# Stick-breaking attention: suffix sums as one-pass products of a rounded part and its remainder, scores with 128 rows of weights, first two heads begun among the projections

## The reference

```python
z = jnp.einsum('bhqd,bshd->bhqs', q_blk, k) * d ** -0.5
causal = key_pos[None, :] < q_pos[:, None]
log_beta = jax.nn.log_sigmoid(z)
log_1m_beta = jnp.where(causal, jax.nn.log_sigmoid(-z), 0.0)
between = lax.cumsum(log_1m_beta, axis=3, reverse=True) - log_1m_beta
w = jnp.where(causal, jnp.exp(log_beta + between), 0.0)
return jnp.einsum('bhqs,bshd->bqhd', w, v)
```

## Time and profile before

| | us |
|---|---|
| median of 3 runs (2274.93 to 2283.06) | 2282.37 |
| the profiled execution | 2286.35 |
| its span | 2284.5 |
| TensorE busy | 2074.4 |
| VectorE busy | 1025.5 |
| ScalarE busy | 756.0 |
| GpSimd busy | 160.6 |
| granted TensorE clock, mean (1 is 2.4 GHz) | 0.94 |

### The profile page before, as it was taken

The page is one execution under the profiler, slowest core; times in us unless marked ns, Lnnn a source line. Parts: engine busy times, 40 slices in busy tenths (PEclk is TensorE's granted clock), DMA queues, the critical chain, the costliest instruction groups (busy, mean ns, idle before and its releaser), DMA issues.

```text
span 2284.5 us, 25379 instructions
## 1 busy us (share of the span) xinstructions
PE 2074.4 (91%) x9952; PEld 1680.9 (74%) x9952; DVE 1025.5 (45%) x1428; ACT 756.0 (33%) x1130; POOL 160.6 (7%) x179
## 2 busy tenths in 40 slices
PE   7999899999998989999999979895459788999898
PEld 6855678887887777788887868683359566888786
DVE  5322534334246554333343345556533437666534
ACT  3134432222235445322223241424213224333322
POOL 3000010000003110100000050000012021000000
PEclk9989899999999998899999989997579899999998
DMA  6200023222222010222222323020020022332231
GB/s 188 93 19 1 19 74 110 92 92 92 93 85 71 27 56 1 76 92 92 92 93 91 101 67 100 1 92 19 19 56 1 1 74 74 99 97 98 74 108 38
DMA packets 140699, 158.09 MB, mean 69 GB/s; under 512 B 15944, under 2 KB 129616, under 8 KB 140624
## 3 DMA queue, kind: packets, MB, share of 16 engines
q1 hardware_dynamic: 139328, 155.01, 21.5%
q0 software_dynamic: 1296, 2.05, 0.3%
HBM read 153.36 MB, written 3.68 MB: 69 GB/s over the span
## 4 chain that ended last, share of the span: by engine, by line
PE 86%; DVE 8%; ACT 2%; issue 2%; POOL 1%; DMA 1%; SPq 0%; DVEq 0%; ACTq 0%; POOLq 0%
PE bank L2373 30%; PE bank L2027 16%; PE bank L2394 16%; PE bank L2051 3%; PE bank L2114 3%; PE bank L2142 2%; PE bank L2239 2%; PE bank L2130 1%; PE bank L2352 1%; PE bank L2227 1%; POOL arena L774 1%; PE bank L2250 1%; PE bank L2562 1%; PE bank L2288 1%; PE bank L2185 1%
## 5 line engine op out<-in xcount | busy, mean ns | idle before, releaser
L2373 PE MATMUL bank<-XH,w_hi 128*128 128x512 f32 x1008 | 398.5, 395 | 0.8 <-DVE w_lo L1569 0.8
L2373 PE MATMUL bank<-XH,w_lo 128*128 128x512 f32 x1008 | 393.4, 390 | 0.0
L2373 PE MATMUL bank<-XL,w_hi 128*128 128x512 f32 x1008 | 393.2, 390 | 0.0
L2027 PE MATMUL bank<-XH,w_hi 128*128 128x512 f32 x528 | 213.1, 404 | 11.9 <-DVE XL L1978 6.5
L2373 PEld LDWEIGHTS bank<-XH,w_hi 128*128 128x128 f32 x1008 | 189.3, 188 | 42.2 <-DVE w_lo L1569 1.6
L2394 PE MATMUL bank<-XH,w_hi 128*128 128x512 f32 x528 | 207.4, 393 | 12.9 <-DVE XL L1556 12.9
L2373 PEld LDWEIGHTS bank<-XH,w_lo 128*128 128x128 f32 x1008 | 189.2, 188 | 39.8
L2373 PEld LDWEIGHTS bank<-XL,w_hi 128*128 128x128 f32 x1008 | 189.4, 188 | 38.8 <-issue 0.5
L2027 PE MATMUL bank<-XH,w_lo 128*128 128x512 f32 x528 | 208.3, 395 | 0.0
L2027 PE MATMUL bank<-XL,w_hi 128*128 128x512 f32 x528 | 208.2, 394 | 0.0
L2394 PE MATMUL bank<-XL,w_hi 128*128 128x512 f32 x528 | 207.1, 392 | 0.0
(11 more groups left out here) (369 smaller groups left out, 3210.6 us busy)
## 6 DMA issues: line engine op xcount, KB each, us to landing
w_raw<-in_ffn_w_gate SPq DMA_DIRECT2D x22, 1024.0 KB, 5.4
w_raw<-in_ffn_w_up SPq DMA_DIRECT2D x22, 1024.0 KB, 5.3
w_raw<-in_ffn_w_down SPq DMA_DIRECT2D x22, 1024.0 KB, 4.9
w_raw<-in_w_up SPq DMA_DIRECT2D x22, 1024.0 KB, 5.1
w_raw<-in_w_in SPq DMA_DIRECT2D x13, 1024.0 KB, 5.3
w_raw<-in_w_down SPq DMA_DIRECT2D x11, 1024.0 KB, 4.9
w_raw<-in_even_w_in SPq DMA_DIRECT2D x9, 1024.0 KB, 5.5
w_raw<-in_even_w_out SPq DMA_DIRECT2D x4, 1024.0 KB, 4.9
```

Source lines behind the costliest of these rows:

```text
L2027: m = pe.matmul(bank[L % 4][0:M, :], cols(w, k), x[:, x0 + k, :], start=(first_k and k == 0 and j == 0), stop=(last_k and k == kt - 1 and ...
L2373: m = pe.matmul(bank[b][:, :], w[:, k, P * c:P * (c + 1)], x[:, k, :], start=(k == 0 and j == 0), stop=(k == KT - 1 and j == 2))
```

## The change

1. The softplus of a head is rounded into an fp32r copy, and the remainder goes into a second one (`two_parts`). A suffix product with blocks e of 0, 1 or 2 becomes two fp32r products, on the copy and on the remainder, with fp32r constants `neg`; those with e = 3 stay f32.
2. The key tiles hold one head each, on 128 partitions of which the other 64 are zero (`key_tiles`; GpSimd zeroes them), so the weights of z have 128 rows. Each key tile is evacuated by two instructions.
3. z(0) goes before `even_qb`, z(1) and suffix(0) between `even_qb` and `even_kvb`. Even heads use banks 4 to 6, odd heads 0 to 2, outputs 7 and 3, `even_kvb` banks 3 and 7. The flips go behind the second key unit and the first value unit (two each, banks 4 and 7).
4. The positions are loaded after the scores, since their place is used meanwhile.

```diff
+        key_tiles = [kTa[:, h, :] for h in range(4)] + [arena[:, base0 + 512 * h:base0 + 512 * (h + 1)] for h in range(4)]
...
+        SBSET = ((4, 5, 6), (0, 1, 2))
+        SBOUT = (7, 3)
+        KVB = (3, 7)
...
+            pool.wait_ge(turned, 9)
+            pool.wait_ge(sq_used, KT)
+            for parity in range(2):
+                rows = slice(64 - 64 * parity, 128 - 64 * parity)
+                link(pool.memset(key_blocks[0][rows, parity:4:2, :], 0.0))
+                pool.memset(key_blocks[1][rows, parity:4:2, :], 0.0).then_inc(keys_zeroed, 1)
...
+                split(qb[0] + 1)
+                ln_part(0)
+                split(qb[1] + 1)
+                split(kvb + 1)
+                ln_part(1)
                 stick_breaking()
...
+            def two_parts(h):
+                if h >= 2:
+                    dve.wait_ge(sb_sum, h - 1)
+                at = sp_high[h % 2]
+                link(dve.tensor_copy(under_arena[:, at:at + 1280], SBL[:, h % 3, :]))
+                for lo, n, to in ((0, 512, sp_low[h % 2][0]), (512, 768, sp_low[h % 2][1])):
+                    last = dve.tensor_tensor(under_arena[:, to:to + n], SBL[:, h % 3, lo:lo + n],
+                                             under_arena[:, at + lo:at + lo + n].bitcast(F32), ALU.subtract)
+                last.then_inc(sb_sp, 1)
...
-                            dve.tensor_tensor(kTa[:, 2 * (j - 2) + t, :], b[:, :], rstd, ALU.mult).then_inc(lin_free, 1)
+                            h = 4 * (j - 2) + 2 * t
+                            dve.tensor_tensor(key_tiles[h][0:64, :], b[0:64, :], rstd[0:64, :], ALU.mult)
+                            dve.tensor_tensor(key_tiles[h + 1][64:128, :], b[64:128, :], rstd[64:128, :], ALU.mult)\
+                                .then_inc(lin_free, 1)
...
+                    pe.matmul(o[:, c:c + SEQ - P * j], key_tiles[h][:, P * j:P * (j + 1)], qTa[:, h // 2, P * j:SEQ],
+                              start=(j != 3), stop=True, skip_group_check=True)
...
+                        if e == 3:
+                            m = pe.matmul(to, C("neg_suffix" if e == j else "neg_ones"), SBL[:, h % 3, at:at + n],
+                                          start=False, stop=True, skip_group_check=True)
+                            continue
+                        low = sp_low[h % 2][0] if e == 0 else sp_low[h % 2][1] - 512 + at
+                        for part in (sp_high[h % 2] + at, low):
+                            m = pe.matmul(to, neg[:, 0 if e == j else 1, :], under_arena[:, part:part + n],
+                                          start=False, stop=True, skip_group_check=True)
...
-                z(0)
-                z(1)
-                for h in range(8):
+                z(2)
+                for h in range(1, 8):
                     suffix(h)
-                    if h >= 1:
-                        values(h - 1)
+                    values(h - 1)
...
+                pe.wait_ge(winbias_ready, 4)
+                z(0)
                 for part, u in enumerate(tok_units("even_qb")):
...
                 L += 4
+                pe.wait_ge(lin_free, L)
+                z(1)
+                suffix(0)
                 u = tok_units("even_kvb")[0]
```

More of the change, by code:

```diff
@@ L212, in build @@
         ARENA = 101 * 256
+        with nc.sbuf_tensor("under_arena", [P, ARENA], F32R) as under_arena:
+            pass
         arena = sb("arena", [P, ARENA])
@@ L980, in even_turned, with ln_part @@
                 act.activation(XH[:, 4 + t, :], bank[at][:, :], ACT.Copy).then_inc(ot_hi, 1)
-            def stick_breaking():
[L983 to L991, removed]
+            def ln_part(h):
+                act.wait_ge(sb_z, h + 1)
+                if h >= 3:
+                    act.wait_ge(sb_o, h - 2)
+                for b, (lo, n) in enumerate(((0, 512), (512, 512), (1024, 256))):
+                    last = act.activation(SBL[:, h % 3, lo:lo + n], bank[SBSET[h % 2][b]][:, 0:n], ACT.Abs)
+                link(last)
+                link(act.activation(SBL[:, h % 3, :], SBL[:, h % 3, :], ACT.Exp, scale=-1.0))
+                act.activation(SBL[:, h % 3, :], SBL[:, h % 3, :], ACT.Ln, bias=1.0).then_inc(sb_ln, 1)
+            def stick_breaking():
                 def weights(h):
@@ L1033, in even @@
                 reciprocal_root("even")
-                for u in qkv[1:] + tok_units("even_qb") + tok_units("even_kvb"):
+                qb, kvb = tok_units("even_qb"), tok_units("even_kvb")[0]
+                for u in qkv[1:]:
                     split(u + 1)
+                split(qb[0] + 1)
[3 more added lines that the diff above has]
+                ln_part(1)
                 stick_breaking()
@@ L1519, in even @@
                 split(qb[0] + 1)
+                softplus(0)
                 split(qb[1] + 1)
+                two_parts(0)
                 for t in range(4):
@@ new lines, in z @@
+            def z(h):
+                if h >= 2:
+                    pe.wait_ge(sb_w, h - 1)
+                for j in (0, 1, 3, 2):
+                    bk, c = SBANK[j]
+                    o = bank[SBSET[h % 2][bk]]
+                    pe.matmul(o[:, c:c + SEQ - P * j], key_tiles[h][:, P * j:P * (j + 1)], qTa[:, h // 2, P * j:SEQ],
+                              start=(j != 3), stop=True, skip_group_check=True)
+                    m = pe.matmul(o[:, c:c + P], identB[:, :], masks[:, 1, :], start=False, stop=True,
+                                  skip_group_check=True)
+                m.then_inc(sb_z, 1)
@@ new lines, in suffix @@
+            def suffix(h):
+                pe.wait_ge(sb_sp, h + 1)
+                for j in (0, 1, 3, 2):
+                    bk, c = SBANK[j]
+                    o = bank[SBSET[h % 2][bk]]
+                    for e in range(j, 4):
+                        n, at = SEQ - P * e, SBOFF[e]
+                        to = o[:, c + P * (e - j):c + SEQ - P * j]
+                        if e == 3:
[6 more added lines that the diff above has]
+                                          start=False, stop=True, skip_group_check=True)
+                m.then_inc(sb_sum, 1)
@@ L2310, in even @@
                         columns("even")
+                    if j in (3, 4):
+                        pe.wait_ge(bias_back, 128)
+                        if j == 4:
+                            pe.wait_ge(winbias_ready, 2)
+                        for w in (2 * j - 6, 2 * j - 5):
+                            pe.matmul(bank[(4, 7)[w % 2]][:, :], C("flip"), winrev[:, 2 * w:2 * w + 2, :],
+                                      start=True, stop=True).then_inc(bias_turned, 1)
+                pe.wait_ge(winbias_ready, 4)
+                z(0)
                 for part, u in enumerate(tok_units("even_qb")):
```

121 lines of the change are left out of this document (55 added, 66 removed).

## The result

The changed kernel takes 2257.64 us (median of four runs, three of them between 2254.97 and 2260.03), the kernel before 2282.72 us on the same chip. The ratio is 0.9893, with a 95% interval from 0.9861 to 0.9925: faster by 24.4 us, from 17 to 32. Forecast were 2262.5 us, with a range from 2251 to 2272.

The account below looks back on a forecast made before the run. TensorE, busy 2074.4 of 2284.5 us, was taken as the bound. Its terms summed to 112.3 us against 134.41, 22.1 less, or 20 net of the clock dip and zeroing: 2262.5 us, range 2251 to 2272.

Parts of the forecast that it names:

- rival 4: Whole change: VectorE's copy at double rate and clock held to the end, 24 us gained, 2258.5 us; chance 0.10.
- Suffix sums: TensorE, per head: one-pass products cut the suffix sums from 4.49 to 2.8 us, 1.7 less.
- Scores: TensorE, z of each head: 128-row weights cut it from 3.48 to 2.65 us, 0.83 less.
- Rival 1: Scores z: weight loads stay exposed with 128 rows, z no cheaper, stretch 6 us longer, 2268.5 us; chance 0.10.
- VectorE's new work: VectorE, per head: a 1.3 us copy and 1.6 us of differences join softplus, 4.6 us with links instead of 1.6.
- The pace: Steady heads: a loop through TensorE, ScalarE and VectorE takes 16.8 us for two heads, 8.4 for one, before 10.27.
- the wait for weights(1): TensorE before z(3): waits 0.6 us, since ScalarE does its 4.0 us for head 2 first, then 1.4.
- The waits: TensorE: 1.0 us before z(1), 0.7 for last value tile, 0.6 for weights(1), 0.75 before steady heads, 3.2 before suffix(7).
- The zeroing on GpSimd: Beside VectorE's split at 29.07, for which TensorE waits: costs 0.2 us (0 to 1).
- The dip behind the last wait: After the 3.2 us wait before suffix(7): the clock dips for some 3.5 us, 1.8 us lost.
- The clock's 8.4 us: First two heads: 8.4 us regained, half of 16.8 at 1.2 GHz, their work lying between dense products at 2.4.
- Rival 3: Steady heads: clock falls to 1.2 GHz, a head 15.5 us instead of 8.4, up to 2308 us; chance 0.07.

Follow-up runs that it names:

- high_first: Changed kernel with each suffix sum doing rounded-copy and f32 products first, waiting only for the copy, and remainder products last: 2255.34 us, ratio 0.9888.
- only_early: Kernel before plus only the early start of the first two heads (new flips, banks and zeroing kept), 64-row scores, f32 suffix sums: 2278.81 us, ratio 0.9989.
- only_rows: Kernel before plus only the 128-row scores (new flips, banks and zeroing kept), f32 suffix sums, heads after the projections: 2269.64 us, ratio 0.9954.
- rows64: Changed kernel with scores on 64 rows of the same key tiles again: 2272.15 us, ratio 0.9962 to the kernel before.
- only_parts: Kernel before plus only two parts and one-pass suffix products (new flips, banks and zeroing kept), 64-row scores, late heads: 2278.58 us, ratio 0.9985.

## Why the prediction was right, and where it was not

The time, the sign and the outline were right. The case that came in its details is one to which I had given only 0.10: rival 4, the copy at double rate and the clock held to the end, with 24 us. The steps:

- *Suffix sums* 2.8 us: measured 2.93 to 2.96. 384 columns cost 0.17 as taken; a product of 256 columns costs 0.16 in front of an f32 one, not 0.12 (145.24 to 145.56 for two).
- *Scores* 2.65 us: measured 2.60. A mask costs 0.06 us, not 0.10. The row of the banded score was the right one to go by. Rival 1, and the rule of the Trainium skill that led to it (TensorE: Matmul & The Clock Gate, "The mechanism"), fell: a score of 512 columns with 128 rows takes 0.94 to 0.96 us, where the columns are 0.90 and 64 rows took 1.06, so the loads are nearly hidden. The same section of the Trainium skill also lets a load run ahead into a background weight buffer, which I had left out; no run here shows whether that is the way.
- *VectorE's new work*: the term that was mis-sized. From the start of softplus to the suffix sums it takes 4.13 us (155.28 to 159.41), not 4.6 and a handing over. The copy of 1280 columns takes 0.83 us, not 1.3:

```profile
155.28 1.62 DVE L1477 SCALAR_TENSOR_TENSOR arena<-bank,arena 128x512 f32<-128x512 f32 x3 [4.04 <-ACT arena L1012]
156.94 0.83 DVE L1485 CAST under_arena<-arena 128x1280 fp32r<-128x1280 f32 x1
157.80 1.56 DVE L1487 TENSOR_TENSOR under_arena<-arena,under_arena 128x512 fp32r<-128x512 f32 x2
```

  The row I called nearest, L1920, was not: it is a copy that also swaps the two dimensions of its source (`XTs.rearrange("p a b -> p b a")`), at 1.0 ns a column, and this copy, which reads its columns in order, runs at 0.65. A nearer row was in the trace of the kernel before, 512 columns in 0.43 us, which scaled by columns gives 1.07 us for 1280:

```profile
L1673 DVE COPY arena<-arena 128x512 f32<-128x512 f32 x1 | 0.4, 427 | 0.7 <-ACT arena L875 0.7
```

  By the Trainium skill (VectorE: DVE Perf Modes, "The perf-mode tier table") the estimate was 0.8 us, and the trace agrees.
- *The pace*: the loop over two heads, forecast 16.8 us, measured 16.24, and shown by the doubled copy to be a real limit. It is not the only one. z, ScalarE's passes and its weights of the other head close a loop of the same length: 2.60 + 0.26 + 3.88 + 1.34 = 8.1 us, from

```profile
151.28 1.36 ACT L1009 ACTIVATE arena<-bank 128x512 f32<-128x512 f32 x3 [2.90 <-PE bank L2276]
...
155.16 1.34 ACT L1018 ACTIVATE arena<-bank 128x512 f32<-128x512 f32 x3
```

  to z at 156.55. I had priced that queue only once, as the wait for weights(1), and rival 1's case was the only one in which I counted it per head. With `high_first`, which relaxes the first loop, it holds the 8.12 us alone.
- *The waits*: 0.78, 0.44, 0.19, about 0.26 and 2.79 us, forecast 1.0, 0.7, 0.6, 0.75 and 3.2. All in the right place and all too long, the last two by VectorE's overpriced copy.
- *The zeroing on GpSimd*: 0.2 us forecast, nothing found. The split beside it takes 2.29 us. In the earlier trace rows it takes 2.55, beside the last sum of squares on GpSimd; the next split of the kernel before takes 2.28.
- *The dip behind the last wait*: 1.8 us forecast, none. The clock is 1.00 from 66 to 230 us. I took the row of a dip after 1.70 us for the effect of the wait. Here 2.79 us did nothing, and in the banded attention of the changed kernel two waits of 1.70 us (before 215.03 and 224.71) left the clock at 1.00 too. So a wait alone does not decide it; what else does was not tested.
- *The clock's 8.4 us*: **right number, wrong reason.** I wrote that this work "would lie between dense products". `only_early` puts it there, and the clock falls all the same; `only_rows` leaves it where it was, and the clock holds. The 128 rows hold it. That the 8.4 us came back all the same is luck, since the place that was to bring them back does not. The early place has another worth: it covers the wait of 5.56 us that the parts would else cause before the first suffix sums, and the half-clock stretch behind it.
- *Rival 3*, the clock falling in the steady heads, did not come. In `rows64` and `only_parts` it did, in part. The rival was a real one for this kernel without its second part; my argument against it, that suffix and values in each head keep the clock up, held for 64-row scores only in the kernels whose suffix sums were long f32 products.

The sum: the stretch was 4.9 us shorter than forecast (24.9 gained, 20 forecast). 1.8 is the dip; 0.8 lies ahead of the tick at 92.33, 3.1 us later than in the earlier trace rows where I had 3.7 for the flips and 0.2 for the zeroing; 4 x 0.28 = 1.1 is the steady heads; 6.25 - 4.46 = 1.8 the waits. Together 5.5, and 0.6 goes back to products that were longer than priced, the suffix sums above all.

## What to carry to other kernels

Ask of each part of a change what it does to the clock when it stands alone. Three parts were worth 1.5, 12.7 and 3.5 us alone here and 24.9 together. The one-pass products add work on VectorE before the first suffix sums, and only the early start of the first heads hides it: those two gave 5.0 us as a sum and 14.0 as a pair. So try the parts alone, in pairs and left out one by one, before one of them is dropped as worthless. When a faster engine meets a loop through other engines, work out every loop through the same queue, and look for the second one that is just as long: it tells how little the next improvement of the first will give. And a price for a copy is scaled only from a row that reads its operands in the same order.

## What the runs showed of the hardware

- f32 scores on 64 rows cost 1.06 us for 512 columns, and 0.16 us from a mask to the next of them; on 128 rows, half of them zeros, 0.94 in `only_rows` (131.45 to 132.39, the mask behind it) and 0.06.
- Two such 64-row products in different halves of the array run side by side: 1.06 us for both.
- With 64-row scores the granted clock often fell to 0.50: in z(1) of `only_early`, 2.7 us after its first score, from dense products at 1.00 and with no wait above 0.8 us before it, and in steady heads (`rows64`, `only_parts`). It did not always: z(0) and z(1) of `rows64` stayed at 1.00, and so did the steady heads of the kernel before.
- With 128-row scores it held, in the stick-breaking stretch, through waits of 2.79 and 3.11 us and fell with one of 5.56. In the banded attention, whose scores have 128 rows too, it fell after shorter ones (at 240.8 in the kernel before, behind 1.70 us).
- A copy from f32 to fp32r of 1280 columns takes 0.83 us on VectorE; a split of 2048 columns beside GpSimd's zeroing was no slower (2.29 us against 2.28 for the next split of the kernel before).
